# Attention and projection in one stage of a hybrid encoder step: how the projection's portions are dealt out along the attention's units

## The reference

```python
# differential attention on the prompt: 4 heads, two score components of 32 channels each
s = jnp.einsum('bqhcd,bkhcd->bchqk', qb, k_all).astype(f32) * scale
s = s + jnp.transpose(bias, (2, 0, 1)).astype(f32)
p = _masked_softmax(s, _chunk_mask(qp, kpos))
w = p[:, 0] - lam * p[:, 1]
o = jnp.einsum('bhqk,bkhd->bqhd', w, v_all)
...
# gated delta rule: projection columns, causal depthwise convolution of width 4, SiLU
y, conv_new = _causal_dwconv(xqkv, conv_buf, conv_w)
y = jax.nn.silu(y)
```

## Time and profile before

| | |
|---|---|
| median of 3 runs | 4552.51 us (4550.89 to 4554.66) |
| the profiled execution | 4545.0 us, its span 4543.2 us |
| PE busy | 3982.9 us, 88% of the span |
| DVE, ACT, POOL busy | 42%, 26%, 17% |
| mean granted PE clock | 0.89 of full speed |
| the stage in layer 1 | 170.2 to 481.4 us |
| the stage in layer 2 | 2398.4 to 2706.9 us |

### The profile page before, as it was taken

The page is one execution under the profiler, slowest core; times in us unless marked ns, Lnnn a source line. Parts: engine busy times, 40 slices in busy tenths (PEclk is TensorE's granted clock), DMA queues, the critical chain, the costliest instruction groups (busy, mean ns, idle before and its releaser), DMA issues. The chain is left out here.

```text
span 4543.2 us, 52378 instructions
## 1 busy us (share of the span) xinstructions
PE 3982.9 (88%) x21722; PEld 3520.2 (77%) x21722; DVE 1898.0 (42%) x3051; ACT 1180.4 (26%) x2113; POOL 778.4 (17%) x622
## 2 busy tenths in 40 slices
PE   4988799889798999999879869998897799999996
PEld 2866587559588999999867646854896799999995
DVE  3243143345424445444434423432553344444444
ACT  2344212323213121212134431232331222121211
POOL 1100010001113222322121000100111223232320
PEclk8987587879799999999989876987898899999998
DMA  3110111010011111111021110110101011111111
GB/s 146 60 34 26 43 63 67 22 57 1 21 33 36 42 38 38 42 42 38 24 104 51 40 53 15 63 53 21 58 2 39 27 39 42 41 38 38 42 42 46
DMA packets 63487, 196.23 MB, mean 43 GB/s; under 512 B 26597, under 2 KB 29157, under 8 KB 59593
## 3 DMA queue, kind: packets, MB, share of 16 engines
q1 hardware_dynamic: 63240, 192.79, 12.7%
HBM read 155.12 MB, written 35.29 MB: 42 GB/s over the span
## 5 line engine op out<-in xcount | busy, mean ns | idle before, releaser
L240 PE MATMUL PS<-h_split,w_split 128*128 128x384 f32 x3072 | 1072.1, 349 | 47.9 <-PEq L179 47.9
L242 PE MATMUL PS<-h_split,w_split 128*128 128x384 f32 x3072 | 1050.8, 342 | 0.0
L241 PE MATMUL PS<-h_split,w_split 128*128 128x384 f32 x3072 | 1047.2, 341 | 0.0
L235 POOL TENSOR_TENSOR w_split<-w_full,w_split 128x1024 fp32r<-128x1024 f32 (+1 forms) x196 | 495.7, 2530 | 1744.8 <-ACT w_split L227 1742.8
L240 PEld LDWEIGHTS PS<-h_split,w_split 128*128 128x128 f32 x3072 | 592.0, 193 | 89.8 <-issue 87.7
L241 PEld LDWEIGHTS PS<-h_split,w_split 128*128 128x128 f32 x3072 | 587.1, 191 | 0.4 <-issue 0.3
L242 PEld LDWEIGHTS PS<-h_split,w_split 128*128 128x128 f32 x3072 | 587.0, 191 | 0.0
L227 ACT CAST w_split<-w_full 128x1024 fp32r<-128x1024 f32 (+1 forms) x196 | 204.6, 1055 | 903.6 <-PE PS L242 760.7
L240 PE MATMUL PS<-ffn_act,w_split 128*128 128x384 f32 x1056 | 367.9, 348 | 71.7 <-DVE x L1945 54.5
L1945 DVE TENSOR_TENSOR x<-x,PS 128x384 f32<-128x384 f32 x528 | 287.0, 552 | 236.8 <-PE PS L242 236.6
L241 PE MATMUL PS<-ffn_act,w_split 128*128 128x384 f32 x1056 | 365.6, 346 | 0.0
(11 more groups left out here) (332 smaller groups left out, 5997.3 us busy)
## 6 DMA issues: line engine op xcount, KB each, us to landing
w_full<-in_w_up SPq DMA_DIRECT2D x88, 512.0 KB, 3.5
w_full<-in_w_down SPq DMA_DIRECT2D x44, 512.0 KB, 3.5
w_full<-in_w_in SPq DMA_DIRECT2D x40, 512.0 KB, 3.7
x_keep<-x SPq DMA_DIRECT2D x2, 4608.0 KB, 19.9
x<-x_keep SPq DMA_DIRECT2D x2, 4608.0 KB, 14.9
w_full<-in_w_out SPq DMA_DIRECT2D x16, 512.0 KB, 3.5
gdn_y<-y_keep SPq DMA_DIRECT2D x2, 3456.0 KB, 14.1
y_keep<-conv_acc SPq DMA_DIRECT2D x12, 512.0 KB, 2.8
```

What stands on the lines that cost most here:

```text
L235: pool.tensor_tensor(ws[:, n % SSLOTS, 1, 0:w], wf[:, n % WSLOTS, 0:w], ws[:, n % SSLOTS, 0, 0:w].bitcast(F32), ALU.subtract).then_inc(w_l ...
L240: pe.matmul(out, w_hi, a_hi, start=first, stop=False)
L241: pe.matmul(out, w_hi, a_lo, start=False, stop=False)
L242: return pe.matmul(out, w_lo, a_hi, start=False, stop=last)
```

## The change

```diff
-            def both(a, b):
-
-                while True:
-                    live = [g for g in (a, b) if next(g, None) is not None]
-                    if not live:
-                        return
+            fill = [0]
+            for i, hh in att:
+                fill += [1, 1, 0] if i < 4 else [1, 1, 1, 1]
+            fill.append(0)
+
+            def both(attention, projection):
+
+                for n in fill:
+                    next(attention)
+                    for _ in range(n):
+                        next(projection, None)
+                for _ in projection:
+                    pass
+                assert next(attention, None) is None
```

## The result

With the change the kernel takes **4609.52 us** (median of 4 runs, 4601.69 to 4620.88); the kernel before takes 4553.59 in the same batch (4 runs, 4550.89 to 4565.04). The ratio is 1.012, with a 95% interval of 1.009 to 1.015: slower by more than the runs scatter, 56 us by the medians.

What follows compares the result with a forecast made beforehand. PE was taken as the bound, busy 88% of the span. Per layer -5.9 + 4.0 + 4.8 + 7.5 + 6.5 = +16.9 us, plus 8 for the clock: 25, 50 for two, on the median 4603 us; range 4562 to 4655.

Steps and rivals of the forecast that it cites:

- Early units, waits: PE's waits before early scores, after one product item per unit leaves: new waits 22.0 us against 11.1 old, per layer.
- Early units, time: Early stretch per layer, without the clock: -16.8 for sixteen items, +22.0 new waits, -11.1 old ones, giving -5.9 us.
- 13 us lost early (10): Clock estimate for the early stretch: 13 us per layer lost to reduced clock after the change, 10 before.
- Early units, apart from the clock: Early stretch per layer, clock left out: -5.9 us.
- SiLU late: Late units: SiLU and two table loads behind the second turned copy, wait 4.3 instead of 3.5 us, five units, +4.0 us.
- Weight split late: Late units: split behind the second turned copy enters the chain with 0.95 us, waits 1.2 to 1.8, five units, +4.8 us.
- Middle and last stretch as time: Late and last units per layer: +4.0 SiLU, +4.8 weight split, +7.5 added products; clock losses 24 (16) and 19 (21) us.
- The last units: Attention's last units: 16 products come in, +16.8 us, of which 9.3 fill existing waits, so +7.5 us per layer.
- rival 2: Faster: added products keep the last units warm, early units keep their 0.91; at 16 us lost, 4533 us. Chance 0.07.
- a sign against me: Last stretch: the prediction is wrong if its clock rises above 0.85 with the middle unchanged.
- The end: After the attention's last copy: last product's copy, table load, SiLU and stores precede the stage's barrier, +6.5 us per layer.
- Clock in all: Whole stage: 56 us instead of 46.6 lost to reduced clock per layer, counted as +8 us.

Runs made afterwards that it cites:

- experiment 1: Changed kernel, with PE alone doing the second item of each early unit behind the turn instead of behind the values: 4561.89 us, 1.002 of the kernel before.
- experiment 2: Changed kernel plus six unread matmuls on PE after the turn of units 0 to 14: 4588.75 us, ratio 1.007 to the kernel before.
- experiment 3: Changed kernel with its first item moved from behind scores 1 to behind scores 0, on all engines: 4597.33 us, ratio 1.011 to the kernel before.
- Experiment 4: Changed kernel with SiLU and weight split of late units back between the two turned copies, on ACT alone: 4583.54 us, ratio 1.006 to the kernel before.
- experiment 7: Changed kernel with PE's early cover, leading item and ACT's earlier end, plus SiLU and weight split ahead of both turned copies: 4513.71 us, 0.991 of the kernel before.
- experiment 5: Changed kernel with ACT's last twelve items ahead of the copies of the attention's last values: 4591.25 us in a single run.

## Why the prediction was right, step by step

Total and sign were right: 4603 forecast, 4609.5 measured. The waits of PE came out nearly term by term. The clock did not: its loss in the early units was put far too small, in the middle and last stretch too large.

In the mean of the two layers the stage grew by 32.6 us: 14.5 in the early stretch, 12.0 in the middle and last together, 6.1 at the end. So both theories of the experiments have a part in it.

- **Early units, waits.** Forecast 22.0 us, with both SiLUs; measured 21.8 in 17 waits, of 0.7 to 1.6 and two of 2.6 and 2.9 behind the SiLUs (units 9 and 15). Right. Experiments 1 and 2 show that they come from the missing cover.
- **Early units, time.** Here the step failed. The forecast for the stretch was -5.9, plus 3 us more lost to the clock. Measured are +11.6 and +17.3. The term that was mis-sized is "13 us lost early (10)": time multiplied by (1 - clock) is 125.4 x 0.27 = 33.9 us and 128.8 x 0.28 = 36.1. Filling the waits with spare matmuls brought the clock to 0.97 and took 20 us out (experiment 2). I had counted on waits of 1.3 us and more for the loss of speed, in 9 early units instead of 5. Measured are 6 such waits among the 17, hardly more than before, and yet the clock fell: much of the speed was lost beside waits of 0.7 to 1.2 us, at the start after one of 1.17. I had left out what the missing first item, ahead of the second scores, opens (experiment 3: 4 to 19 us of the stretch). The first four units were to shorten by 0.1 to 0.3 us each and took 4.7 us more together; at full clock, in experiment 3, they take 2.1 less than before (14.1 against 16.2).
- **Early units, apart from the clock.** By the prediction's own factor of 0.88 the clock accounts for 20.9 and 23.9 us of the change. That leaves -9.3 and -6.6 us, where -5.9 was forecast: as an estimate, this part of the sum was right.
- **SiLU late.** Forecast a wait of 4.3; measured 4.0 to 4.5 in units 18, 21, 24 and 27. Behind unit 30 there are no more scores, and the wait of 4.5 us stands before unit 31's turn, for DVE. Right.
- **Weight split late.** Forecast 1.2 to 1.8 in units 17, 20, 23, 26, 29; measured 1.0 to 1.7. Right as a wait. Experiment 4 confirms where both waits come from: they are 3.3 to 3.8 and 0.4 to 0.7 us there.
- **Middle and last stretch as time.** The two can't be set against the terms one by one, because with the new order a SiLU's wait before unit 28's scores has moved from the middle to the last stretch. Together the terms are 4.0 + 4.8 + 7.5 = 16.3, and 5.2 more for the clock (43 us lost instead of 37): 21.5. Measured are 11.8 and 12.2. The term that is too large is the clock's: 20.4 us lost in the middle (136.1 x 0.15) and 10.0 in the last (71.5 x 0.14), 30.4 instead of 43. Without the clock's share the change is 18.8 and 16.9, near the 16.3. In experiment 4, 4.9 us less of waiting came with 4 us more lost to the clock; where the waits fall by 8 us, from 21.9 to 13.5, and none is over 1.9, the clock rises to 0.92 and the middle gives 13 us (experiment 7).
- **The last units.** The clock rose to 0.86 from the 0.69 and 0.67 of the earlier trace rows: 10.0 us lost where 19 were forecast. The first half of rival 2 is real: the products do keep the last units warmer. What I had named as a sign against me, a clock above 0.85 there with the middle unchanged, was met in layer 1 (0.86, and 0.85 in the middle after 0.86). It didn't turn the change into a gain, since the loss moved to the early units, which this rival let keep their 0.91.
- **The end.** Forecast +6.5, measured +6.1; the next stage's table load starts at 514.20 beside its first DMA, hidden, and experiment 5 took 2.9 us of the gap away by moving the SiLU.
- **Clock in all.** Forecast 56 us lost per layer; measured 33.9 + 20.4 + 10.0 = 64.3 and 36.1 + 20.4 + 10.0 = 66.5. The stage as a whole grew by 29.5 and 35.6 us instead of 25. Taken apart by the factor of 0.88, the clock has 13.8 and 19.3 of it (8 forecast), everything else 15.7 and 16.3 (16.9 forecast). Outside the stage the profiled span grew by 6 us more (71.1 - 65.1); that part of the program is the same in all twelve kernels and took between 3921 and 3932 us. The medians grew by 56.

The total was near because an underestimate of some 18 us in the early stretch stood against an overestimate of 9.5 in the middle and last. It was right in its kind, and partly by luck in its size.

Open remains in which pattern of waits the clock falls and when it comes back. With the changed kernel's code the early stretch took 119.6 to 130.4 us in the different runs, the middle 135 to 142 and the last 71.5 to 79.1, at different clocks; what picks one value is not shown. The changed kernel's own two early passes are among the slowest of the six, so part of its 56 us may be this scatter. Gains and losses below some 10 us per layer should for that reason be read in the stretch that was edited, and not in the total.

## What to carry to other kernels

Deal filler work by where the chain on the other engines is open, not by equal counts: here one item in each early unit, moved from behind the values to behind the turn on PE, was worth 48 us of the kernel's time. Take operations that switch ACT's table, with their reload, out of the chain between two steps of the bounding engine, and let nothing but landed stores stand between the last step and a stage's barrier. Before moving work out of a stretch, ask what the stretch's clock does with the gaps that remain.

## What the hardware showed unexpectedly

- Useless matmuls saved time: 180 more of them, 21 us less (experiment 2). The granted clock of the early stretch rose from 0.73 to 0.97, and the stretch with less work was the slower one.
- A single wait of 1.2 us, in the midst of thin work, was followed by 0.60 up to unit 4 (0.59 to 0.90 in the six passes over that code); the same units with waits of 0.7 only kept 1.00. The Trainium skill says in "TensorE: Matmul & The Clock Gate", section "What's actually happening", that the throttled state is the default and activity releases it. The trace agrees where work was put into the waits: 0.73 became 0.97 in experiment 2. The share of busy time alone doesn't order the stretches, though: PE is busy for 83% of the early stretch both in the changed kernel, at 0.73, and in experiment 1, at 0.88.
- A table load takes its 1.28 us and no more of ACT's time: the load starts at 406.10, the SiLU at 407.39, and the reload at 408.59 is followed by the exponential at 409.89. What makes it expensive is only who waits for ACT.
